# GpSimd held back at the feed-forward boundaries, more squares added on VectorE, and sums of squares by 64 columns of ones

## The reference, cut to what matters

```
rms_norm_2(x, g): y = xf * rsqrt(mean(xf*xf, axis=-1) + 1e-6) * g
swiglu(x, w_in, w_out): a, b = split(x @ w_in); (silu(a) * b) @ w_out     # D_FF = 2816

first block, second half:
h2 = rms_norm(x, g_norm2) * (1 + sc2) + sh2 ;  x = x + gt2 * hier_moe(h2)
second block:
h = h + 0.5 * rms_norm_2(swiglu(rms_norm_2(h, g_ffn1_pre)), g_ffn1_post)
h = h + rms_norm_2(mixer(rms_norm_2(h, g_mix_pre)), g_mix_post)
h = h + 0.5 * rms_norm_2(swiglu(rms_norm_2(h, g_ffn2_pre)), g_ffn2_post)
```

## Time and profile before

| | us |
|---|---|
| median of 3 runs (2158.42 to 2165.49) | 2161.84 |
| the profiled execution itself | 2168.82 |
| its span in the profile | 2166.8 |
| TensorE (PE) busy | 2078.1 (96%) |
| VectorE (DVE) busy | 1279.4 (59%) |
| ScalarE (ACT) busy | 833.1 (38%) |
| POOL busy | 788.1 (36%) |

### The profile page before, as it was taken

One profiled execution on the slowest core, in us unless ns is written; L12 is line 12 of the kernel. 1 busy time (PEld: TensorE's weight loads), 2 busy tenths in 40 slices (PEclk: granted clock), 3 DMA queues, 4 the chain that ended last, 5 costly groups with the idle time before them and its releaser, 6 DMA issues.

```text
span 2166.8 us, 31293 instructions
## 1 busy us (share of the span) xinstructions
PE 2078.1 (96%) x12492; PEld 1777.2 (82%) x12492; DVE 1279.4 (59%) x1959; ACT 833.1 (38%) x1018; POOL 788.1 (36%) x595
## 2 busy tenths in 40 slices
PE   4999999999999999979999999999999998999998
PEld 4698787888767666669999999888878788999997
DVE  7375476555465656477677676332431358777775
ACT  7441255222345555344333333343332234333332
POOL 1341233444300000036556552221244435656660
PEclk7898999999989999979999998999999999999999
DMA  9122213555317999712322221111123212223321
GB/s 266 39 79 72 85 59 98 188 191 171 110 59 262 337 342 344 248 59 89 107 97 97 97 97 39 59 59 59 59 78 98 78 59 78 98 97 106 107 97 59
DMA packets 175760, 261.12 MB, mean 121 GB/s; under 512 B 12233, under 2 KB 140922, under 8 KB 175662
## 3 DMA queue, kind: packets, MB, share of 16 engines
q1 hardware_dynamic: 174126, 257.65, 35.8%
q10 hardware_dynamic: 1536, 2.10, 0.3%
HBM read 257.62 MB, written 2.11 MB: 120 GB/s over the span
## 4 chain that ended last, share of the span: by engine, by line
PE 86%; DVE 7%; ACT 4%; issue 1%; POOL 1%; DMA 1%; SPq 0%; DVEq 0%; POOLq 0%; ACTq 0%
PE PS L798 64%; PE PS L1355 7%; PE PS L1395 5%; PE PS L1524 1%; DVE Hf L2368 1%; ACT mod_early L1725 1%; PE PS L892 1%; PE PS L885 1%; DVE Hf L2338 1%; POOL w_lo L727 1%; PE PS L1328 1%; PE PS L1476 1%; DMA mod_early<-in_w_mod 1%; PE PS L905 1%; PE PS L1036 0%
## 5 line engine op out<-in xcount | busy, mean ns | idle before, releaser
L727 POOL TENSOR_TENSOR w_lo<-w_raw,w_hi 128x512 fp32r<-128x512 f32 x444 | 595.5, 1372 | 1287.0 <-ACT w_hi L1703 1265.0
L798 PE MATMUL PS<-HH,w_hi 128*128 128x512 f32 (+2 forms) x1408 | 471.3, 346 | 23.7 <-DVE HL L2291 7.9
L798 PE MATMUL PS<-HL,w_hi 128*128 128x512 f32 (+2 forms) x1408 | 467.3, 343 | 0.0
L798 PE MATMUL PS<-HH,w_lo 128*128 128x512 f32 (+2 forms) x1408 | 465.7, 342 | 0.0
L1703 ACT ACTIVATE w_hi<-w_raw 128x2048 fp32r<-128x2048 f32 x133 | 254.8, 1916 | 392.0 <-DVE w_raw L2329 147.9
L798 PEld LDWEIGHTS PS<-HH,w_hi 128*128 128x128 f32 x1408 | 264.0, 192 | 61.7 <-issue 21.3
L798 PEld LDWEIGHTS PS<-HH,w_lo 128*128 128x128 f32 x1408 | 263.9, 192 | 30.8
L798 PEld LDWEIGHTS PS<-HL,w_hi 128*128 128x128 f32 x1408 | 263.5, 192 | 30.0
L738 POOL TENSOR_TENSOR wx_lo<-wx_raw,wx_hi 128x512 fp32r<-128x512 f32 x132 | 190.0, 1467 | 6.5 <-DVE Hf L2338 6.5
L2867 DVE TENSOR_TENSOR m_lo<-m_raw,m_hi 128x2048 fp32r<-128x2048 f32 x56 | 128.5, 2297 | 76.8 <-ACT m_hi L2030 76.6
L3129 DVE TENSOR_TENSOR yacc<-yacc,PS 128x528 f32<-128x528 f32 (+1 forms) x176 | 117.8, 691 | 49.4 <-PE PS L798 48.6
(11 more groups left out here) (498 smaller groups left out, 4087.1 us busy)
## 6 DMA issues: line engine op xcount, KB each, us to landing
w_raw<-in_w_in SPq DMA_DIRECT2D x49, 1024.0 KB, 5.1
w_raw<-in_w_ffn_in SPq DMA_DIRECT2D x44, 1024.0 KB, 4.8
m_raw<-in_w_exp_gate SPq DMA_DIRECT2D x56, 512.0 KB, 4.3
m_raw<-in_w_exp_up SPq DMA_DIRECT2D x56, 512.0 KB, 5.4
m_raw<-in_w_exp_down SPq DMA_DIRECT2D x56, 512.0 KB, 4.8
w_raw<-in_w_ffn_out SPq DMA_DIRECT2D x22, 1024.0 KB, 4.8
mod_late<-in_w_mod SPq DMA_DIRECT2D x16, 1024.0 KB, 5.2
mod_early<-in_w_mod SPq DMA_DIRECT2D x8, 1024.0 KB, 11.9
```

The costliest lines, as they stand in the source:

```text
L727: ins = pool.tensor_tensor(w_lo[:, s, cs], w_raw[:, s, cs], w_hi[:, s, cs].bitcast(F32), ALU.subtract)
L798: ins = mm(o, l, r, **k)
```

## The change

`SQ_DENSE` becomes 0, so VectorE adds all eight tiles of squares in the norms that use it; the norm before feed-forward 1 keeps two tiles on TensorE under the new name `SQ_UNSORT`. All sums of squares multiply by 64 equal columns of ones instead of one; ScalarE's root reads every 64th column. `norm` gets a parameter `hold`: so many identity products (8, and 0 for the paced norms) stand ahead of the wait for the total of squares. POOL waits for that total before it splits anything of feed-forward 1, and for the four block sums before it splits the extra blocks of up 0; at the mixer it waits for the total of the norm behind feed-forward 1 ahead of the first chunk, and for that of the next norm ahead of the third. In the first unit of each feed-forward `weight_sums` of up 1 moves ahead of `block_sums(actf)`. In the last norm the rows of token groups 2 and 3 move wholly behind the sums, and groups 0 and 1 keep their first half ahead.

```diff
-SQ_DENSE = 2
+SQ_DENSE = 0
+SQ_UNSORT = 2
+WIDE = 64
...
-            def split_seven(c, s, more=0, sums=None):
+            def split_seven(c, s, more=0, blocks=None):
-                if sums is not None:
-                    pool.wait_ge(sqsum_ready, sums)
+                if blocks is not None:
+                    pool.wait_ge(t_ready, blocks)
...
-                split_seven(c, c % RING, sums=2 if n == 0 else None)
+                if n == 0:
+                    pool.wait_ge(sqsum_ready, 2)
+                split_seven(c, c % RING)
-                split_seven(c + 1, (c + 1) % RING)
+                split_seven(c + 1, (c + 1) % RING, blocks=4 if n == 0 else None)
...
-            rounds = (FF_AT[1] - mixer_at) // RING
+            pool.wait_ge(sqsum_ready, 3)
+            for c in range(mixer_at, mixer_at + RING):
+                if c == mixer_at + 2:
+                    pool.wait_ge(sqsum_ready, 4)
+                split_chunk(c, c % RING)
+            rounds = (FF_AT[1] - mixer_at) // RING - 1
-                    split_chunk(mixer_at + s, (mixer_at + s) % RING, i)
-            for c in range(mixer_at + RING * rounds, FF_AT[1]):
+                    split_chunk(mixer_at + RING + s, (mixer_at + s) % RING, i)
+            for c in range(mixer_at + RING * (rounds + 1), FF_AT[1]):
...
-            def sum_squares(T, own):
+            def sum_squares(T, own, hold):
+                        keep_clock(hold, s)
-                        ins = mm(PS[0:G, s, 0, j:j + 1], Hf[:, k, G * j:G * j + G], ones[:, 0:1],
+                        ins = mm(PS[0:G, s, 0, WIDE * j:WIDE * j + WIDE], Hf[:, k, G * j:G * j + G], ones[:, 0:WIDE],
...
-            def norm(T, own, idle):
-
-                s = sum_squares(T, own)
+            def norm(T, own, hold, idle):
+
+                s = sum_squares(T, own, hold)
...
-            norm(SEQ, SQ_DENSE, 5)
+            norm(SEQ, SQ_DENSE, 8, 5)
...
-            norm(TALL, SQ_DENSE, 20)
+            norm(TALL, SQ_UNSORT, 8, 20)
-            norm(TALL, SQ_DENSE, 28)
-            norm(TALL, SQ_PACED, 20)
+            norm(TALL, SQ_DENSE, 8, 28)
+            norm(TALL, SQ_PACED, 0, 20)
...
-            norm(SEQ, SQ_DENSE, 28)
-            norm(SEQ, SQ_PACED, 20)
+            norm(SEQ, SQ_DENSE, 8, 28)
+            norm(SEQ, SQ_PACED, 0, 20)
+
...
-            for k in range(SQ_DENSE):
-                pe.wait_ge(sq_ready, hcount["sq"] + k + 1)
-                for j in range(NTOK):
-                    mm(PS[:, s, 0, j:j + 1], Hf[:, k, P * j:P * j + P], ones[:, 0:1], start=k == 0 and j == 0, stop=False,
-                       skip_group_check=True)
-            for k in range(4):
-                W.wait_released(downs_at + k)
-                for t in range(NTOK):
+            for t in range(2):
+                for k in range(4):
+                    W.wait_released(downs_at + k)
-                ins = mm(PS[:, s, 0, j:j + 1], Hf[:, SQ_DENSE, P * j:P * j + P], ones[:, 0:1], start=False, stop=True,
+                ins = mm(PS[:, s, 0, WIDE * j:WIDE * j + WIDE], Hf[:, SQ_DENSE, P * j:P * j + P], ones[:, 0:WIDE], start=j == 0, stop=True,
-                for k in range(4, KT):
+                for k in range(4 if t < 2 else 0, KT):
...
-                W.release(af(rsc[0:G, 0:J], PS[0:G, s, 0, 0:J], ACT.Sqrt, scale=1.0 / D, bias=eps[0:G, 0:1]))
+                W.release(af(rsc[0:G, 0:J], PS[0:G, s, 0, 0:WIDE * J:WIDE], ACT.Sqrt, scale=1.0 / D, bias=eps[0:G, 0:1]))
...
-                if m > SQ_DENSE + 1:
-                    add_square(Hf, TALL, m - 1, SQ_DENSE)
+                if m > SQ_UNSORT + 1:
+                    add_square(Hf, TALL, m - 1, SQ_UNSORT)
...
+                weight_sums(at_ + 3)
-                weight_sums(at_ + 3)
...
-            norm(TALL, every, c2(0), SQ_DENSE, split="blocks", while_summed=lambda: clear_y(TALL, 0, 4),
+            norm(TALL, every, c2(0), SQ_UNSORT, split="blocks", while_summed=lambda: clear_y(TALL, 0, 4),
...
-                if m > SQ_DENSE + 1:
+                if m == 4:
+                    for k in range(SQ_DENSE + 1, 4):
+                        add_square(Hf, SEQ, k, SQ_DENSE)
+                if m > 4:
```

## The result

The changed kernel takes 2153.56 us (median of 10 runs, 2148.81 to 2159.12) against 2165.22 us (10 runs, 2158.42 to 2171.55) of the kernel before on the same chip: ratio 0.9943, 95% interval 0.993 to 0.9957, 12.3 us less by the ratio (the medians are 11.7 apart). The profiled executions have spans of 2149.2 and 2166.8 us. Of the 17.6 us between them some 6 are a slow execution before (2168.82 us against the median of 2165.22) and a quick one after (2150.95 against 2153.56).

What follows compares the result with a forecast made beforehand. The prediction took TensorE as the bound nearly everywhere (86% of the chain of waits), with gains only from the seven norms. Its terms summed to -12.8 us, 2161.84 to 2149 us, range 2142 to 2160.

Steps and rivals of the forecast that it cites:

- Norm before the experts: Fills keep the clock full, so total of squares to multiplication takes 2.8 us instead of 5.1: -2.3 us.
- rival A: In the norms, the clock falls as before despite fills and 64 columns: -4.2 us, 2157.6 us; chance 0.20.
- Norm before feed-forward 1: Holding POOL starts VectorE's block stage 4.8 us earlier, but POOL takes up to 4.4 back: -1.2 us taken.
- First units: First units of both feed-forwards: new waits for block sums, old waits gone; +0.5 and -1.3, together -0.8 us.
- Pair ahead of the mixer: Two norms behind feed-forward 1: -4.5 us at full clock, -2.0 with it lost in one; -3.3 taken.
- Two more additions ... I take +0.4: Behind feed-forward 1, VectorE's two extra additions wait for ScalarE, making the total 0 to 0.8 us later.
- POOL's hold costs nothing that I can find: At the mixer, delaying POOL's chunk splits until the totals of squares costs no time: 0 us.
- Rest of feed-forward 1: Feed-forward 1 behind gate 0 of its first unit: new block-sum wait against old waits removed, +0.5 us.
- Pair ahead of feed-forward 2: Two norms behind the mixer: -2.3 us in the dense one, -0.3 in the paced one, -2.6 together.
- last norm: Final norm: sums follow the total at once, with groups 2 and 3 moved behind them: -2.6 us.
- B: First units lose to new waits and half clock, feed-forward 1's norm gains 0: -9.9 us, 2152 us; chance 0.14.
- C: Fills end early, the clock falls, paced sums run slowly (+7.6 and +4.2): +2.0 us, 2164 us; chance 0.06.

Runs made afterwards that it cites:

- columns only: The kernel before with sums of squares multiplied by 64 columns of ones instead of one, and nothing else changed: 2156.73 us, ratio 0.9953.

## Why the prediction was right, and where not

**Norm before the experts, -2.3: the size right, the reason not.** The clock held, and every duration of the sum was met. I gave it to the fills and said that widening costs nothing and, in rival A, does nothing. The fills do hold the clock with one column (1.50 us idle, 1.05 us for 8 passes), but in the change they only make good for the two tiles' sums that were taken away; 64 columns without fills and with these sums do the same (0.85 us idle, 2.9 us to the multiplication). In rival A I used the Trainium skill, "TensorE: Matmul & The Clock Gate", section "Back-to-back issue gap": a free dimension of 1 and of 64 takes the same cycles. That the two take the same time agrees with the runs (60 passes in 4.82 us with one column, in 4.88 with 64). That the widening alone would do nothing was my inference, and it fell: columns only, 0.9953.

**Norm before feed-forward 1, -1.2.** The total came 3.5 us earlier as worked out (+7.68 to +4.22 us), and POOL took back what it gave: four of VectorE's block operations take 2.3 us and three 1.9, for the usual 1.2. The prediction's own sum was loose there: 6 x 1.1 less 1.6 is 5.0, more than the 4.8 us that it set against them, and not 4.4. Net -0.7, and by the run with POOL as before none of that is the hold's; what remains is the 12 passes of the total at full clock (1.18 us in that run, 1.92 before).

**First units, -0.8.** In the changed kernel TensorE waits for the block sums 2.0 and 2.1 us (predicted 2.4), and not for POOL. Feed-forward 2: -1.5 for -1.3. In feed-forward 1 the first pair of units took 0.4 us longer, as predicted, but the half-clock stretch behind the old wait, 1.7 us, is gone in this trace; I had named that only as an end of the range.

**Pair ahead of the mixer, -3.3: the step that failed.** Measured +0.3 between the two traces. The step is "TensorE is idle about 1.6 us ahead of the first total", and with it the full clock in one of the two norms at the price of the other. Three parts. (1) "Two more additions ... I take +0.4": 1.6 us, from 3.3 to 4.9 us where POOL is held and from 4.2 to 5.9 where it isn't, since VectorE's next instruction needs ScalarE's second square. (2) The last products of feed-forward 1 ran 1.7 us of work slower before, at half clock, while ScalarE's chunk landed at the same time; once they are fast, the squares are late by them (ScalarE's split of the chunk begins 6.6 us ahead of the last product, before 8.0): 1.4 us given back. The run with only the last norm changed shows this by itself: full clock there, and the old total 4.3 us behind in place of 2.9. POOL's hold saves 1.0 of it. (3) So TensorE was idle 3.10 us, not 1.6, and the fills couldn't bridge it: 6.0 us to the multiplication in place of 3.2. Of the two norms only the second was fast, 3.8 us for 6.0. "POOL's hold costs nothing that I can find" is wrong for the variants, where it costs 0.8 us at the first new square. In the changed kernel POOL is done at 1334.76, before the additions to the residual begin at 1336.42, and it costs nothing.

The mechanism failed in every trace that has it: three have these instructions and this hold (3.10, 3.12 and 3.25 us idle), and in each the clock fell before the multiplication, though not at the same place; in the second the 12 passes still ran at full:

```profile
1335.09 1.15 PE L913 MATMUL PS<-ones,Hf 128*88 128x64 f32 x12 [3.12 <-DVE Hf L2342]
```

How much the step missed by is less sure. The pair took 33.2, 31.7 and 32.2 us in these three, and 32.9 and 37.0 in the two traces with the old instructions, so the gain lies anywhere from -5.3 to +0.3 us.

**Rest of feed-forward 1: a term that I left out.** -4.6 us where I had +0.5. POOL's hold at the mixer shortens the wait for the low activations from 2.0 to 0.5 us; that is the term, and both runs without the hold show it. Another 1.7 us are the half clock behind the old wait (3.4 us long), which only two of five traces with that wait have, so it is chance as much as the change. The last 1.7 are the stretch at 1003 to 1007, behind POOL's other wait. The prediction looked at POOL's hold only for what it delays and not at what POOL had been disturbing. That the sum came out is in part luck: between these two traces a gain of 4 to 5 us unforeseen stands beside 3.6 us not made, and both figures hang on where the clock fell in the trace of before.

**Pair ahead of feed-forward 2, -2.6, and last norm, -2.6.** -3.9, of which the pair itself has -2.3: the dense norm gave its 2.2 us, the paced one 0.9 in place of 0.3, as its end isn't half-clocked, and the three additions cost 0.9 us at the total, where I had none. The other 1.5 us lie in gate 0 behind it: 15.4 us in the trace of before, with a half-clock stretch at 1805 to 1809, 15.4 also with the weight sums as before, and 13.9 us in all the others, the one with only the last norm changed (and so the old order) among them. That trace says that they need not be of the change. Last norm -2.1: order alone, as the run shows; 0.5 less because the first 16 passes wait 0.89 us for ScalarE's rows of the residual and end at 2138.95, where the sums could have begun at 2138.18.

**The rivals.** A is refuted for the norm before the experts, holds behind feed-forward 1, and behind the mixer the clock was kept in four of six traces. B's new waits are there. The half clock behind them isn't in the changed kernel's trace, but it is in 3 of 10 in feed-forward 1 and in 4 of 10 in feed-forward 2, and POOL did take back all that the hold gave before gate 0 was done. C's slow paced sums are real: once behind fills that ended 1.70 us early, with one column, and in the old pair with only the last norm changed, there with no idle time ahead of them. Its price was added up wrongly: 9.6 - 4.82 - 0.6 is 4.2 and not 7.6, so by its own rows the clock lost in both norms gives -1.4 us, and it never reaches "slower". The Trainium skill, "SBUF — State Buffer", section "Who interferes with whom", says that VectorE with two inputs in SBUF contends with GpSimd's reads; the trace agrees in the two places compared (0.69 against 1.78 us, 1.25 against 2.33).

**Still open.** Why two programs with the same instructions around the pair keep the clock in one trace (1.44 us idle) and lose it in the other (1.59), or behind the mixer keep it in four traces and lose it in two, all with 1.50 us idle. Which widths between 1 and 64 would do was not tried. And the times tell variants apart by no less than 0.15 to 0.2%, the width of the intervals to either side; what the traces give below that (fills, POOL's holds, the order of the weight sums) stands on one profiled execution each.

## What to carry to other kernels

Where small products only reduce over partitions, make them wide even if the extra columns are thrown away: it is a small edit, the passes take no longer (0.080 and 0.081 us), and 10.2 of the 12.3 us came with it alone. Before work is taken from TensorE ahead of a wait, count the idle time that it leaves and who computes it instead; two additions more on VectorE made the total behind feed-forward 1 come 1.6 us later, and the clock fell ahead of the multiplication in all three traces of that (31.7 to 33.2 us for the pair). Without them it was kept there in three of four; with the fills behind the spread made longer too, the pair took 29.3, 29.4 and 31.6 us, and with 28 of them 34.3. And when a stall on one engine goes, look at what was landing at a fixed time in its shadow, since that can become the next wait, as ScalarE's split of the late chunk did here.

## What the runs showed of the hardware

Passes over 1 and over 64 columns take the same time (0.080 and 0.081 us), but the granted clock treats them differently: behind 0.90 us of idleness 8 passes over one column ran at 0.50, behind 0.85 us 8 passes over 64 columns at 1.00, in otherwise equal programs (two traces with one column, four with 64, the norm before the experts).

Idleness ahead of the first total behind feed-forward 1, in the eleven traces with 64 columns: 0.80, 0.86, 1.05 and 1.44 us left the clock full; at 1.59 and 3.12 it fell behind the passes, at 3.25 within them, and at 2.43, 3.10, 4.17 and 5.08 us it was down when they began. That 3.10 and 3.12 us, behind equal instructions, differ in this shows that the length of the idle stretch doesn't settle it. These are rows of one place and no rule.
